# The even mixer of a hybrid decoder trunk, rewritten as one stream of projections with the recurrence steps at fixed places in it

## What is computed

```python
def gla_ssd_mixer(h, w_in, gla_w_gate2, gla_b_gate2, gla_norm_w, conv_w, conv_b, dt_bias, a_log, d_skip, ssm_norm_w, w_out):
    q, k, v, g, a_low, z, xbc, dt = jnp.split(h @ w_in, points, axis=-1)
    log_a = jax.nn.log_sigmoid(a_low @ gla_w_gate2 + gla_b_gate2) / GLA_GATE_NORMALIZER
    o = gla_chunked(q, k, v, log_a)                      # 4 heads, dk 128, dv 256
    o = rmsnorm(o, gla_norm_w) * jax.nn.silu(g)
    xbc = jax.nn.silu(causal_depthwise_conv(xbc, conv_w, conv_b))   # width 4
    xs, bm, cm = jnp.split(xbc, ...)
    dt = jax.nn.softplus(dt + dt_bias)
    y = ssd_chunked(xs * dt, dt * -jnp.exp(a_log), bm, cm) + d_skip * xs   # 16 heads in 4 groups
    y = rmsnorm(y * jax.nn.silu(z), ssm_norm_w)          # per group of 256 columns
    return jnp.concatenate([o_gla, y], axis=-1) @ w_out
```

## Time and profile before

| | us |
|---|---|
| median of 3 runs | 2365.56 (2363.37 to 2369.52) |
| the profiled execution, its own time | 2367.07 |
| its span, first to last instruction | 2365.3 |
| TensorE busy in the span | 2239.2 (95%) |
| VectorE, ScalarE, GpSimd busy | 1009.8, 739.3, 193.0 |
| the even mixer's inner part, 412.70 to 997.77 | 585.07 |

### The profile page before, as it was taken

How to read it: one execution, slowest core, us unless ns; L and a number is a source line. 1 busy time by engine, 2 the same in 40 slices (tenths; PEclk the granted TensorE clock), 3 DMA queues, 4 the chain that set the end, 5 groups by cost and what they waited for, 6 DMA issues and landing times.

```text
span 2365.3 us, 25040 instructions
## 1 busy us (share of the span) xinstructions
PE 2239.2 (95%) x10358; PEld 1812.3 (77%) x10358; DVE 1009.8 (43%) x1438; ACT 739.3 (31%) x1141; POOL 193.0 (8%) x128
## 2 busy tenths in 40 slices
PE   7999999798888888999999999999998789999999
PEld 6888888677765666888888888888886348888887
DVE  4333224458876665443332343332265335333322
ACT  4222223433333333332221232222233434322211
POOL 0000001332212120000000000000033000000000
PEclk9999999899998889999999999999999779999999
DMA  5332332221111112242323232323222002332331
GB/s 180 95 102 89 107 98 71 79 71 45 54 36 37 43 36 101 69 134 89 107 89 107 72 125 92 104 89 107 90 83 75 15 0 71 118 106 89 107 98 54
DMA packets 55298, 197.31 MB, mean 83 GB/s; under 512 B 6272, under 2 KB 6784, under 8 KB 55184
## 3 DMA queue, kind: packets, MB, share of 16 engines
q1 hardware_dynamic: 53856, 193.75, 25.4%
q10 hardware_dynamic: 1328, 1.96, 0.2%
HBM read 193.58 MB, written 2.10 MB: 83 GB/s over the span
## 4 chain that ended last, share of the span: by engine, by line
PE 61%; DVE 4%; issue 3%; ACT 2%; POOL 1%; DVEq 0%; ACTq 0%; POOLq 0%
PE ps L789 11%; PE ps L790 11%; PE ps L791 11%; PE ps L797 7%; PE ps L799 7%; PE ps L798 7%; PE ps L1162 1%; PE ps L1161 1%; DVE a_rows L1226 1%; ACT a_rows L415 1%; ACT a_rows L727 1%; DVE a_rows L1223 1%; DVE temps L1223 1%; PE ps L1042 0%; PE ps L1172 0%
## 5 line engine op out<-in xcount | busy, mean ns | idle before, releaser
L789 PE MATMUL ps<-h_hi,w_hi 128*128 128x512 f32 (+1 forms) x1976 | 746.8, 378 | 12.4 <-DVE temps L1599 9.2
L791 PE MATMUL ps<-h_hi,w_lo 128*128 128x512 f32 (+1 forms) x1976 | 734.4, 372 | 0.0
L790 PE MATMUL ps<-h_lo,w_hi 128*128 128x512 f32 (+1 forms) x1976 | 733.9, 371 | 0.0
L415 ACT ACTIVATE w_hi<-raw 128x1024 fp32r<-128x1024 f32 x352 | 370.5, 1056 | 790.5 <-PE ps L799 392.4
L1223 DVE TENSOR_TENSOR w_lo<-raw,w_hi 128x1024 fp32r<-128x1024 f32 x288 | 343.7, 1221 | 338.0 <-ACT w_hi L415 337.4
L789 PEld LDWEIGHTS ps<-h_hi,w_hi 128*128 128x128 f32 x1976 | 376.4, 190 | 86.1 <-issue 21.1
L791 PEld LDWEIGHTS ps<-h_hi,w_lo 128*128 128x128 f32 x1976 | 376.2, 190 | 64.3
L790 PEld LDWEIGHTS ps<-h_lo,w_hi 128*128 128x128 f32 x1976 | 376.6, 191 | 61.8 <-issue 2.5
L1223 DVE TENSOR_TENSOR a_rows<-a_rows,ps 128x512 f32<-128x512 f32 x88 | 60.5, 688 | 614.0 <-PE ps L791 614.0
L797 PE MATMUL ps<-w_hi,a_hi 128*128 128x512 f32 x704 | 274.4, 390 | 0.0
L799 PE MATMUL ps<-w_hi,a_lo 128*128 128x512 f32 x704 | 274.0, 389 | 0.0
(11 more groups left out here) (182 smaller groups left out, 1918.9 us busy)
## 6 DMA issues: line engine op xcount, KB each, us to landing
raw<-in_w_gate_up SPq DMA_DIRECT2D x176, 512.0 KB, 3.7
raw<-in_w_down SPq DMA_DIRECT2D x88, 512.0 KB, 3.5
raw<-in_w_xbc SPq DMA_DIRECT2D x16, 512.0 KB, 3.5
raw<-in_w_zg SPq DMA_DIRECT2D x16, 512.0 KB, 3.5
raw<-in_w_even_out SPq DMA_DIRECT2D x16, 512.0 KB, 3.6
raw<-in_w_qk_small SPq DMA_DIRECT2D x9, 512.0 KB, 3.5
raw<-in_w_v SPq DMA_DIRECT2D x8, 512.0 KB, 3.5
raw<-in_w_odd_out SPq DMA_DIRECT2D x8, 512.0 KB, 3.5
```

The source lines that it names most:

```text
L415: return nc.scalar.activation(to, source, ACT.Copy, scale=scale)
L789: nc.tensor.matmul(to, w_h, hi, start=first, stop=False)
L790: nc.tensor.matmul(to, w_h, lo, start=False, stop=False)
L791: return nc.tensor.matmul(to, w_l, hi, start=False, stop=last)
```

## The change

The even mixer is written anew, and the other sublayers keep their instructions.

- **One stream.** The projections become one generator (`projections`). Its blocks are counted by a "place": places -40 to 0 are the rest of `qk_small`; 0 to 128 `vg` (v and g in four blocks of four slots, tokens on the partitions); then `xbc0`, `z01`, `xbc12`, `z2`, `xbc3`, `z3` up to 320; and 320 to 384 the first half of `even_out`. `project_to(place)` runs blocks up to a place. `plan_even` gives each step a fixed place: heads at 12, 53, 94 and 135, groups at 176, 221, 266 and 311.
- **Splits.** `split_to(place)` on ScalarE and VectorE splits slots as far as the ring of four allows at that place. GpSimd makes no `w_lo` in this mixer any more; VectorE makes them all. GpSimd keeps the eight powers. ScalarE and VectorE call `split_to` (in `keep_up`) at the place of each step.
- **Token-major rows.** v, g and z lie with tokens on the partitions. The norms' sums come from ScalarE's accumulator, and VectorE scales by a column; the sums and the spread on TensorE go, and eight transposes for each head or group (`turn_head`, `turn_group`) come in. `cat` is split straight from these transposes in PSUM, head by head.
- **Convolution from PSUM.** ScalarE makes the first tap (and bias) of every tile out of PSUM, VectorE adds three taps out of PSUM; the copy is gone, and a bank is free only behind the last tap (`conv_done`).
- **Takes.** ScalarE copies q, k and v out of PSUM and applies SiLU to g and z on the way (`take_blocks`, `take_z`). The scaling by 1/16 of `log_a` moves into the exponentials; `log_decay(h + 1)` runs inside head h, `step_sizes` inside head 0.
- In a group the decays are made by four small products instead of a spread row of ones, and the skip term by eight products.

```diff
+def plan_even():
+    at = {}
+    for h in range(GH):
+        base = 12 + 41 * h
+        for j, step in enumerate((0, 3, 7, 10, 14, 17, 22)):
+            at["level", h, j] = base + step
+        at["own", h], at["far", h], at["out", h], at["head_turn", h] = base + 25, base + 30, base + 36, base + 61
+    for g in range(SG):
+        base = 12 + 41 * GH + 45 * g
+        for name, step in (("x", 0), ("cb", 10), ("skip", 20), ("y_far", 35), ("group_turn", 49)):
+            at[name, g] = base + step
+        for r in range(4):
+            at["decay", g, r] = base + (13, 16, 22, 27)[r]
+            at["near", g, r] = base + (22, 27, 31, 35)[r]
+    tile_end = [128 + 8 * (n + 1) + (32 if n >= 4 else 0) + (16 if n >= 12 else 0) for n in range(16)]
+    return at, tile_end
...
-            split_some("qk_small", INNER, 9)
-            split_some("v", 0, 8)
-            split_some("xbc", 0, INNER)
-            for name, count, norm in (("xbc", GH, ("gla", 0)), ("zg", SG, ("ssm", 0))):
-                for turn in range(count):
-                    for n in range(4):
-                        if n == SPLITS_BEFORE_NORM[name]:
-                            power(turn + norms[norm])
-                        split_low(stages[name][0] + INNER + 4 * turn + n)
+            for n in range(GH + SG):
+                power(n)
...
+        def split_to(place):
+            while upcoming["slot"] < min(stream + place // 8 + 4, INNER_END):
+                split_high(upcoming["slot"])
+                upcoming["slot"] += 1
...
+            def decay_of(j):
+                act.wait_ge(gla_diff, h * 8 + (j + 1))
+                nc.scalar.activation(scaled[j % 2], scaled[j % 2], ACT.Exp, scale=1.0 / 16.0).then_inc(gla_decay, 1)
+            for j in range(len(SPANS)):
+                take_blocks(even_at["level", h, j])
+                decay_of(j)
+                keep_up(even_at["level", h, j])
+                if j == 5 and h:
+                    turn_head(h - 1)
+            take_blocks(even_at["own", h])
...
+        def projections():
+            for n in range(4, 9):
+                if n == 8:
+                    pe.wait_ge(tile_taken, QK0 + 4)
+                yield from tile(first_slot[s] + n, first_bank(n))
+            pe.wait_ge(tile_taken, QK0 + 8)
+            for b in range(4):
+                yield from token_tiles(stream + 4 * b, lambda c: pe.wait_ge(vg_taken, 4 * (b - 1) + c + 1) if b else None)
+            for n in range(4):
+                pe.wait_ge(vg_taken, 12 + n + 1)
+                yield from tile(stream + 16 + n, n)
+            yield from token_tiles(stream + 20, lambda c: pe.wait_ge(conv_done, c + 1))
+            for n in range(8):
+                pe.wait_ge(z_taken, n + 1) if n < 4 else pe.wait_ge(conv_done, n + 1)
+                yield from tile(stream + 24 + n, n % 4)
+            yield from narrow_tiles(stream + 32, lambda c: pe.wait_ge(conv_done, 8 + c + 1))
+            for n in range(4):
+                pe.wait_ge(z_taken, 4 + n + 1)
+                yield from tile(stream + 34 + n, n)
+            yield from narrow_tiles(stream + 38, lambda c: pe.wait_ge(conv_done, 12 + c + 1))
+            yield from first_half(s, block_source, lambda index: pe.wait_ge(cat_lo_ready, index + 1))
+        projecting = projections()
...
+        def head(h):
+            for j in range(len(SPANS)):
+                project_to(even_at["level", h, j])
+                if j == 6 and h:
+                    turn_head(h - 1)
+                pe.wait_ge(gla_factors, h * 8 + (j + 1))
+                if h or j >= 2:
+                    pe.wait_ge(gla_merged, h * 8 + (j - 1))
+                for c in range(NC):
+                    queries = slice(c * HALF_P, c * HALF_P + HALF_P)
+                    last = nc.tensor.matmul(ps[:, 4 + j % 2, queries], k_dec[j % 2][:, c * P:c * P + P], other[j % 2][:, queries],
+                                            start=True, stop=True)
+                last.then_inc(gla_products, 1)
...
+        def split_to(place):
+            while upcoming["slot"] < min(stream + place // 8 + 4, INNER_END):
+                split_low(upcoming["slot"])
+                upcoming["slot"] += 1
...
+                of, row = conv_column(n), rows(a_rows, conv_row(n))
+                dve.wait_ge(conv_started, n + 1)
+                for back in (1, 2, 3):
+                    if back > 1:
+                        dve.wait_ge(conv_step, 2 * n + back - 1)
+                    stt(row[:, back:T], ps[:, n % 4, 0:T - back], conv_w[:, of, 3 - back:4 - back], row[:, back:T],
+                        ALU.mult, ALU.add).then_inc(conv_step if back < 3 else conv_done, 1)
...
+            for j in range(len(SPANS) + 1):
+                if j < len(SPANS):
+                    differences(j)
+                if j == 1 and h:
+                    head_mean(h - 1)
+                if j:
+                    factors(j - 1)
+                if j == 7:
+                    chunks = log_a.rearrange("p (c t) -> p c t", c=NC)[:, 0:3, :]
+                    dve.wait_ge(gla_factors, h * 8 + 7)
+                    tt(scaled[0][:, 0:3 * P].rearrange("p (c t) -> p c t", c=3), chunks[:, :, P - 1:P].to_broadcast([P, 3, P]),
+                       chunks, ALU.subtract).then_inc(gla_diff, 1)
+                if j >= 3:
+                    merge(j - 3)
+                if j == 5 and h:
+                    dve.wait_ge(vg_taken, 8 if h < 3 else 16)
+                    gate()
+                if j < len(SPANS):
+                    keep_up(even_at["level", h, j])
+                if j == 2 and h + 1 < GH:
+                    log_decay(h + 1)
+                if j == 3 and h == 0:
+                    step_sizes()
+                if j == 5 and h == 1:
+                    far_step_sizes()
+            if h:
+                turn_head(h - 1)
```

More of the change, by code:

```diff
@@ new lines, in group @@
+                    last.then_inc(y_far_done, 1)
+                first_four(s)
+                project_to(-32)
+                pe.wait_ge(even_in, 48)
+                pe.wait_ge(small_taken, 1)
+                pe.wait_ge(tile_taken, QK0 + 3)
+                for h in range(GH):
+                    last = nc.tensor.matmul(ps[:, 4 + h, :], gate2[:, h * P:h * P + P], rows(a_rows, SMALL)[A_LOW:A_LOW + RANK, :], start=True, stop=True)
+                last.then_inc(decay_logits, 1)
+                for h in range(GH):
+                    head(h)
@@ L1086, in odd @@
+                for g in range(SG):
+                    group(g)
+                project_to(even_at["group_turn", SG - 1])
+                turn_group(SG - 1)
+                for _ in projecting:
+                    pass
+                second_half(s, block_source)
             def odd():
@@ L1668, in ssm_groups @@
-                    gate(0)
-                    outputs(1)
-                    dve.wait_ge(y_gated, g * 2 + 1)
-                    take(2)
-                    gate(1)
-                    dve.wait_ge(group_squares, g + 1)
-                    tt(square_sum, square_sum, other[0], ALU.add).then_inc(group_summed, 1)
-                    norm(g + norms[("ssm", 0)], 256, head_rstd)
-                    for m in range(2):
-                        row = rows(a_rows, g * 2 + (XS + m))
-                        last = stt(row, row, mixer_cols[:, ds(g * 2 + (94 + m), 1)], head_rstd, ALU.mult, ALU.mult)
@@ L1680, in ssm_groups @@
-                    after(last)
-                    take(3)
-                    for m in range(2):
-                        dve.wait_ge(row_silu, g * 4 + (m + 3))
-                        row = rows(a_rows, g + (Q + GH * m))
-                        last = tt(row, row, scaled[m], ALU.mult)
-                    last.then_inc(group_done, 1)
+                    keep_up(even_at["near", g, 3])
+                    pair = token_pair.rearrange("p (c v) -> p c v", c=2)
+                    dve.wait_ge(y_far_done, g + 1)
@@ new lines, in even @@
+                for buffer in k_dec:
+                    nc.vector.memset(buffer, 0.0)
+                after(nc.vector.memset(temps[:, 6, :], 0.0))
+                dve.wait_ge(dt_act, 1)
+                ts(far2, far1, 1.0, None, ALU.add).then_inc(dt_signal, 1)
+                split_to(-32)
+                logits()
+                split_to(-16)
+                dve.wait_ge(softplus_ready, 1)
+                log_decay(0)
+                split_to(0)
+                for h in range(GH):
+                    head(h)
```

1146 lines of the change are left out of this document (626 added, 520 removed).

## The result

The change takes 2442.02 us (median of 4 runs, 2440.87 to 2444.05) against 2366.37 before: a ratio of 1.032, 95% interval 1.0303 to 1.0338. Of all the executions in this document one, in e7, took 4468.57 us and is left out of its median and ratio. The profiled execution has its own time of 2441.5 and a span of 2439.7. It is 74.4 us longer than the span of before.

| part | before | after | difference |
|---|---|---|---|
| up to the mixer (unchanged code) | 397.1 | 407.3 | +10.2 |
| the even mixer | 610.2 | 644.8 | +34.6 |
| the later sublayers (unchanged code) | 1358.0 | 1387.6 | +29.6 |

A forecast was written before the change was run, and what follows sets the result against it. TensorE waits in the even mixer (72.0 us idle) and its lowered clock were taken as the loss. Idle +42, clock +23 and steps -5 made +60 on 2367.07, 2427, predicted as 2425 us, range 2335 to 2485.

The forecast's parts named there:

- TensorE's work stays: the 61 slots of 24 matmuls at 0.2266 us: Even mixer: TensorE's slot matmuls take 331.7 us both before and after the change.
- The chain at a slot's end: Heads: split, differences and factors queue behind a slot's end, 3.9 to 4.0 us, hidden only by blocks before the level.
- level 2: Head 1: log_decay, 3.6 us in all, stands before this level's factors and leaves TensorE idle 1.5 us.
- the next head's entry: End of head 1: squares, splits, differences and factors start only after the output; five blocks hide 3.4, leaving 3.5 us idle.
- Heads: The four heads together leave TensorE idle about 84 us, against 19.8 before.
- q, k and small columns: First stage of the mixer: all waits go but one for the last tile's copy; 3 us idle left of 13.8.
- Groups: Idle 27 us in place of 37.9, from the last head's gate and turn, z tiles and SiLU of x.
- Clock: Even mixer: 26 waits in place of 15, at 2.7 us of lower clock each, 70 us in place of 47: +23.
- steps -5: TensorE in the even mixer: norm sums and spreads give way to eight transposes, narrow z tiles add 2.6; net -5 us.
- Tables: ScalarE switches between SiLU and exponential cost 1.28 us each when exposed, without the 1.38 more of a drain.
- Engines running ahead: Rival, chance 0.22: a slot's end costs a level under 2 us instead of 4; 2332 us, or some 2260.
- The low clock: Rival, chance 0.22: heads never get back to 2.4 GHz for long; +40 on the forecast, 2465 to 2485 us.

The follow-up runs named there:

- e7: e3 with the next head's logarithmic decay made at a head's end instead of behind level 2's differences: 2355.52 us.
- e2: The change with table mixer_cols 196 columns wide instead of 172, so the rows behind it are back on a multiple of 64 bytes: 2393.26 us.
- e3: e2 with ScalarE and VectorE catching up with their splits four places later in the heads' level passes: 2360.02 us.
- e4: e2 with the low halves of the 22 slots due in the heads made by GpSimd instead of VectorE: 2367.84 us.
- e12: e10 with the late splits undone, so they are again at the level's own place: 2347.59 us.
- e10: e8 with five edits more, each reordering work for one wait seen in its trace; the best version: 2296.89 us.
- e1: The kernel before with table mixer_cols 172 columns wide instead of 132, the new columns unread: 2414.94 us.
- e9: The kernel before with 128 unread bytes ahead of x in SBUF, moving weights, h and a: 2366.69 us.
- e6: e3 with ScalarE taking the turned head behind the last level's exponential instead of ahead of it: 2336.64 us.
- e5: The kernel before with table mixer_cols 148 columns wide instead of 132, moving the rows behind it by 64 bytes: 2390.11 us.
- e8: e3 with the edits of e6 and e7, earlier first differences and exponential of the next head, and later SiLU of group 0's x: 2328.82 us.

## Why the prediction was right, and where it was not

Slower was right, and 2442 lies in the range of 2335 to 2485; the value of 2425 was 17 us short. That nearness is luck: two misses of opposite sign nearly cancel. The rewritten mixer cost 26.9 us (e2) where I said 60, and 48.8 us came from a cause that no step named. On the old boundary the change takes 2393, still slower and in the range, but 32 under the value.

- **The step that failed: "TensorE's work stays: the 61 slots of 24 matmuls at 0.2266 us".** The number of matmuls stayed and their price did not. I had read the table's new width in the diff as forty columns more to store. It moved every row behind it by 160 bytes, and each 512-column matmul took 6.7 to 7.6 ns more, in all sublayers. It is shown in both directions: put into the kernel before (+49.9) and taken out of the change (-48.8).
- **The chain at a slot's end held.** Rows of the change show `w_hi`, `w_lo`, differences and factors in that order, with 3.63 us from the begin of `w_hi` to the end of the factors where the terms of the forecast make 3.69; the merge behind them makes it 4.12. e3, e4 and e12 take the chain apart or put it back, for 33.2, 25.4 and 50.7 us. Head 1 by levels, forecast and measured: level 1 4.0 and 3.8; level 2 1.5 and none; level 4 with its bank 5.0 and 5.7 (4.96 and 0.78); level 5 1.4 and none; level 6 5.0 and 5.8; the next head's entry 3.5 and 2.5. The merge, which I had left out, ends many of the waits, 0.34 us behind the factors.
- **Heads: 84 us of idle time forecast, 70.1 measured.** Head 0 was set too high (24 with the next entry; the change shows 15.7). The terms that were too high are the ones without a slot's end. For level 2 the rows show why: I had priced the four scans of `log_decay` at the mean of the earlier trace rows, 0.75. That mean holds single ones of up to 2.50; the median there is 0.39, and in the change the mean is 0.41, so the four take 1.37 together:

```profile
L1660 DVE TENSOR_TENSOR_SCAN a_rows<-ones,a_rows 128x128 f32<-128x128 f32 x16 | 5.5, 406 | 0.1
547.02 1.37 DVE L1660 TENSOR_TENSOR_SCAN a_rows<-ones,a_rows 128x128 f32<-128x128 f32 x4
```

  With the pass of 0.68 that is 2.05 in place of 3.6, and nothing is left of the 1.5.
- **q, k and small columns: 3 forecast, 5.1 measured**, 4.1 of them behind one tile that ScalarE takes.
- **Groups: 27 forecast, 16.8 measured.** The last head's turn cost 3.5 instead of 4.5 and SiLU of x 1.3 instead of 2.6; the z tiles 0.7 and 0.8 where 2.3 and one or two more each were set. One of 5.1 us that I hadn't named stands ahead of the narrow tiles of the last group, behind a convolution tile; e10 halves it.
- **Clock: 26 waits at 2.7 us, +23 over before.** I count 20 waits of 1.9 us or more in the change. With the address mended, TensorE's busy time of the inner part is 516.1 us, 3 over the 513.1 of before, where steps -5 and clock +23 gave 531. A fixed price per wait is the wrong form: from e2 to e3 idle time falls by 27.2 us and busy time at the same work by 4.0; from e3 to e10 by 34.9 and 29.6. What sets the price stays open.
- **Sum.** Forecast for the inner part 585 + 60 = 645, measured 620.0, and 610.2 on the old boundary. The rest: forecast 0, measured +39.8.
- **Reading of the clock line.** The earlier trace rows has its low slices at 8 and at 13 to 15; slices 9 to 12 are at 9. The sum doesn't use this.
- **Tables.** A load of 1.28 us at 559.58 and the next activation at 560.87: again no drain, so the value of the row was the one to take.
- **Rivals.** Engines running ahead: a slot's end was to cost a level under 2 us, and costs about 4. The low clock: 0.82 in the heads, but without the 40 us more: TensorE's busy time of the inner part is only 3 us over before (e2). The signs named beforehand came: waits of 4 us at slot ends, a head of 65 to 78 us between entries, a clock under 0.85, GpSimd idle, no wait over 3 us just ahead of `even_out`.

In the later sublayers e1 lost 35.6 us and the change 29.6, with the same address. The difference lies in the other mixer alone. Its windows before, in e1 and in the change (cut at the same blocks of transposes):

```profile
1735.70:2006.65 270.95, 240.21 (x972) 162.94 (x971) 119.50 (x209) 98.94 (x216) 41.43 (x25) 0.88 0.15 49
1769.98:2045.10 275.12, 245.67 (x973) 165.03 (x971) 117.36 (x209) 99.31 (x216) 41.74 (x25) 0.87 0.16 49
1801.52:2070.51 268.99, 239.31 (x973) 161.80 (x971) 117.34 (x209) 99.21 (x216) 41.74 (x25) 0.90 0.16 50
```

The same instructions take 275.1 us at a clock of 0.87 and 269.0 at 0.90, with 29.5 and 29.7 us idle: this mixer's clock comes out differently from one execution to another (with the spacing of before it takes 269.4 us in e9 and 273.1 in e6). Everything else behind the mixer (three feed-forward parts) loses 31.4 us in e1 and 31.6 in the change.

Left open: what in the hardware the two steps (64 and 128 bytes) belong to, and what sets the clock's price of a wait. No run here looked at either.

## What to carry to other kernels

A change of one small table's width can move every large operand behind it: look at the spacing of matmuls in code that wasn't touched before explaining a difference by the code that was, and keep the rows of both TensorE operands on multiples of 128 bytes. Where an in-order engine catches up with background work at the moment when its input just becomes ready, everything queued behind it waits as well; called four blocks later, the same work cost 33.2 us less in one version of this kernel and 50.7 in another. A wait is paid twice, since TensorE's clock falls behind it, but the second part isn't proportional to the first: one mended chain can give back little of it and the next as much as its waits, so an edit that seems to bring little is better judged again when its neighbours are mended.

## What the runs showed of the hardware that was not expected

- A float32r matmul of 128x128 by 128x512 in a dense stream at 2.4 GHz (granted clock 1.00) starts every 226.7 ns in the kernel before, and as well when h and a are moved by 256 bytes (e2) or all operands by 128 (e9). With h, the moving operand, moved by 64 bytes it is 228.9 (e5), by 160 bytes 234.3 (e1). With a, the stationary one, moved by 64 or 160 bytes it is 233.3 (e5, e1). With the place of before taken as a multiple of 128, these are offsets of 0, 64 and 32 from one.
- The lower clock isn't paid wait by wait. Idle time taken from the inner part, and busy time that came back with it at the same work: 27.2 and 4.0 us (e2 to e3), 12.6 and 13.1 (e3 to e6), 16.7 and 15.2 (e8 to e10); put back from e10 to e12, 32.4 and 23.0. The heads' mean granted clock is 0.84 in e2, 0.86 in e3, 0.92 in e6, 0.97 in e10 and 0.86 in e12. Each pair is of two single executions, and the eleven of e3 lie 7.1 us apart, so the 4.0 is uncertain by some microseconds.
